# Splitting the recurrence gates' matrix products of the even layer into three rounded products

## The chip, the core and the metric

The kernel runs as one launch on one core of one Trainium2 chip. The metric is the device time of the launch in microseconds (us). Engines are named as the profile names them: PE (TensorE matmuls; PEld is its weight load, which overlaps), DVE (VectorE), ACT (ScalarE), POOL (GpSimd), SP (SyncE, which here only issues transfers from memory).

## The reference, cut to what matters

The program is a stack of four blocks on 512 tokens of width 1024. Only the first one, the even layer, is touched. For each of 8 heads ("channels" here, 128 wide) it projects the normed input six ways, runs a short convolution over one of them (`ua`), makes four gates out of `ua` with 128x128 matrices, and runs a forward and a backward linear recurrence with them:

```python
def rg_lru(u, gate_w, gate_b, lam, reverse):
    uh = uf.reshape(bsz, seq, RG_HEADS, RG_HEAD_DIM)
    gates = sigmoid(einsum('bshi,ghij->gbshj', uh, gate_w) + gate_b)
    r, i = gates[0], gates[1]
    log_a = -RG_C * r * softplus(-lam)
    a = exp(log_a)
    b = sqrt(-expm1(2.0 * log_a)) * (i * uf)
    ...                                   # h_t = a_t h_(t-1) + b_t

def even_layer(x, ...):
    xa, za, xb, gb, gc, zb = split(rmsnorm(x) @ w_in)
    ua = centred_dwconv(xa, conv_w) + conv_b
    ya = (rg_lru(ua, forward) + rg_lru(ua, backward)) * silu(za)
    yb = gb * centred_dwconv(gc * xb, sc_w) * silu(zb)
    y = concatenate([ya, yb]) @ w_out
```

## The kernel before

**Split products.** Nearly all of PE's work is in products of the form hi·w_hi + lo·w_hi + hi·w_lo: a float32 operand is rounded to a high part (type fp32r) and the remainder is its low part. A weight tile of 128x1024 (a "slot") comes through a ring of four slots; POOL makes its high part (`split_slot`, L332, a CAST) and its low part (L334, a TENSOR_TENSOR) in one of two buffer pairs, and counts `w_ready`. PE counts `slots_used` when a slot is through, after which POOL may write that pair again. So POOL works at most two slots ahead of PE. One slot is 8 k-steps of 3 matmuls, 24 in all.

**Channels.** The even layer is a sequence of 8 channels of 6 slots each (slots 0 to 47 below), each slot one projection. PE works through the slots and then through the four gates of the channel, `even_gates` (L654), written before as plain float32 matmuls on `gw` and `ua` (L660). Only channel 0's gates stand later: behind the first slot of channel 1 (L680). ACT moves each projection out of its bank (L1314) in the order xa, xb, gc, gb, zb, za. DVE makes `ua` out of xa (L1763, L1766), then the second convolution (L1790 to L1800); then, when ACT has made the gates' sigmoids and decays (`decay_ready`), the recurrence (L1806 to L1821), and counts `even_channel_done`. Each engine runs its own program in written order; semaphores join them.

**Channel 0** has extra work on DVE between `ua` and the second convolution (`if c == 0:`, L1770): scaling the first banks, norming the input, and a series for the decay constants (`decay_terms`) in tiny operations.

**Channel 7**, the last, has extra work on DVE in the same place (`if last:`, L1786): 14 low parts `y_low_dve` of outputs that are done already, each of which waits for a high part that ACT makes (`y_highs`, L1320) after its last move of this channel.

**After the channels** PE runs the output product (`EVEN_OUT`, L708 to L710). Its first five output tiles leave out the two parts that need channel 7 (`EVEN_K[-2:]`), which come behind those 5 times 14 k-steps.

**Transfers.** SP issues in this order in its loop: wait until the channel two back is done (`even_channel_done`), the gate tile (L590), then the six weight slots (L587), each when the slot before it in the ring was split. So a channel's first weight slots leave only when DVE has finished the channel two earlier.

Of the kernel before, what the change touches and what calls it, by code (L numbers as in the profile page):

```python
# [6 lines left out]
F32 = mybir.dt.float32  # L7
BF16 = mybir.dt.bfloat16
F32R = mybir.dt.float32r
U32 = mybir.dt.uint32  # L10
ACT = mybir.ActivationFunctionType
ALU = mybir.AluOpType
AX = mybir.AxisListType.X

P = 128
D = 1024
T = 512
# [3 lines left out]
RG_HEADS = 8  # L21
# [9 lines left out]
RING = 4  # L31
HALVES = (12, 10)
SLOT = HALVES[0] * P
# [40 lines left out]
GATE_COLS = 4 * P + 16  # L74

SIGNALS = """
const_landed consts_landed out_stored slots_used split_begun w_ready w_cast
masks_zero log_ready nsp_ready plain_high plain_low plain_scaled even_scaled even_high even_low
even_moved ua_ready gates_done gates_read decay_ready factor_ready root_b_ready even_channel_done y_high y_low y_done yb_done
y_moved res_done x_high x_low square_ready square_added sumsq_ready token_sums root_ready rinv_copied token_root token_rinv rinv_ready  # L80
proj_scaled proj_copied r_moved weights_gained v_copied lr_done lr_copied lr_high lr_ready
# [23 lines left out]
def build(nc, x_in, consts_in, gates_in, weights, out):  # L105
    ctx = ExitStack()
    with ctx:
        sem = {}
# [4 lines left out]
        gate_landed = [ctx.enter_context(nc.semaphore(f"gate_landed_{j}")) for j in range(2)]  # L113

        base = (nc.sbuf_base + 31) // 32 * 32
        place = {}
# [6 lines left out]
        def at(name, cols, start, dt=F32):  # L123
            return nc.alloc_sbuf_tensor_at(name, [P, cols], dt, offset=base + 4 * start)

        def tiled(name, n, cols, start, dt=F32):
            return at(name, n * cols, start, dt)[:, :].rearrange("p (k t) -> p k t", t=cols)
# [6 lines left out]
        ARENA_AT = place["arena"]  # L134
# [5 lines left out]
        ring = tiled("ring", RING, SLOT, place["ring"])  # L140
# [271 lines left out]
        r = Region(0, FREE)  # L412
# [12 lines left out]
        nsp = r.take(16)  # L425
        nsp_c = r.tiles(2, 2)
        lt = r.tiles(6, 16)
        even_tmp = [ps[:, 4 + d, :] for d in range(2)]
        rinv_even = ps[:, 6, :]

# [199 lines left out]
        def _(pe):  # L630
# [22 lines left out]

            def even_gates(i, jj):  # L654

                pe.wait_ge(sem["ua_ready"], 2 * i + (jj + 1))
                pe.wait_ge(sem["gates_read"], 2 * i + (jj + 1))
                pe.wait_ge(gate_landed[jj], 16 * i + 16)
                for g in range(4):
                    mm = nc.tensor.matmul(ps[:, 4 + g, :], gw[:, jj, g * P:(g + 1) * P], ua[:, jj, :],  # L660
                                          start=True, stop=True)
                mm.then_inc(sem["gates_done"], 1)

            def even_channel(i, jj, c=None):
# [622 lines left out]
        def _(act):  # L1287
# [15 lines left out]
            def even_act(i, jj, c=None):  # L1303
# [4 lines left out]
                for n, (dst, func) in enumerate(dsts):  # L1308
                    s = 6 * jj + n
                    if c == 0:  # L1310
                        act.wait_ge(sem["plain_scaled"], n + 1)
                    else:
                        act.wait_ge(sem["slots_used"], 12 * i + used("even_in", s + 1))
                    nc.scalar.activation(dst, ps[:, s % RING, :], func).then_inc(sem["even_moved"], 1)  # L1314
                    if c == 0 and n == 3:
                        for k in range(DT):
                            act.wait_ge(sem["even_scaled"], k + 1)
                            nc.scalar.activation(hi[:, k, :], even_tmp[k % 2], ACT.Copy).then_inc(sem["even_high"], 1)
# [365 lines left out]
        def _(dve):  # L1684
# [43 lines left out]
            def even_dve(i, jj, c=None):  # L1728
# [59 lines left out]
                        y_low_dve(n, k)  # L1788
                moved(3)
                V.tensor_tensor(u_pad[:, 1:1 + T], gc_s[:, jj, :], xb_s[:, jj, :], ALU.mult)  # L1790
                dve.drain()
                V.tensor_scalar(cv, u_pad[:, 0:T], par[:, 9:10], None, ALU.mult)
                for k in range(1, 3):
# [566 lines left out]
        def _(pool):  # L2360
# [6 lines left out]
            pool.wait_ge(sem["w_ready"], ready("even_in", 1))  # L2367
            for j in range(1, RING):
                split_slot(pool, "even_in", 0, j)
            with pool.Fori(0, slots_of["even_in"] // RING - 1) as i:  # L2370
                for j in range(RING):
                    split_slot(pool, "even_in", i + 1, j)
            pool.wait_ge(sem["consts_landed"], 16)
            for dst, name in ((ident_1, "ident"), (causal_1, "causal_neg"), (sb_neg_1, "sb_neg"), (neg_c_1, "neg_c")):
                G.tensor_copy(dst, con(name))
# [229 lines left out]
```

## Time and profile before

| | us |
|---|---|
| median of 3 runs (lowest, highest) | 2743.24 (2742.39, 2743.55) |
| the profiled execution | 2743.05 |
| its span | 2741.2 |
| PE busy | 2701.0 |
| POOL busy | 1629.6 |
| DVE busy | 1321.7 |
| ACT busy | 711.8 |

The profiled execution is 1.85 us longer than its span, which is what lies around it. Starts in the trace are counted from the span's start. The even layer's channels lie between 24 and 309 us.

### The profile page before, as it was taken

How to read it: one execution, taken by the hardware profiler on the slowest of the kernel's cores; microseconds unless marked ns; L12 is line 12 of the kernel's file. 1: busy time of each engine (PE TensorE's matmuls, PEld its weight loads, DVE VectorE, ACT ScalarE, POOL GpSimd, SP SyncE). 2: the span in 40 equal slices, each digit the busy share in tenths (PEclk: the TensorE clock that was granted, in tenths of full speed). 3: DMA queues.
4: the chain of work that ended last, by engine and by line, in shares of the span. 5: the costliest groups of instructions: out<-in, count | busy, mean ns of one | idle time of the engine just before them, and what ended most of it. 6: DMA issues, size and time to landing. Idle time of an engine off the chain costs nothing.

```text
span 2741.2 us, 35951 instructions
## 1 busy us (share of the span) xinstructions
PE 2701.0 (99%) x13142; PEld 2166.8 (79%) x13142; DVE 1321.7 (48%) x1601; ACT 711.8 (26%) x1235; POOL 1629.6 (59%) x947
## 2 busy tenths in 40 slices
PE   9999999999999999999999999999999999999999
PEld 6777777867888888867888888788888766888887
DVE  7878824574532461176440433642244777543242
ACT  4433423343200110284210113310011477211010
POOL 5566755514665666603665666566666799566565
PEclk9999999999999999999999999999999999999999
DMA  4322322202332323301332333433232100233232
GB/s 180 101 93 94 90 92 85 84 24 71 96 118 77 96 96 92 93 9 47 92 109 82 100 100 92 125 98 115 77 107 85 55 1 2 85 99 116 77 97 87
DMA packets 62028, 235.58 MB, mean 86 GB/s; under 512 B 6880, under 2 KB 7008, under 8 KB 61792
## 3 DMA queue, kind: packets, MB, share of 16 engines
q1 hardware_dynamic: 61920, 234.14, 27.0%
q8 instruction: 68, 1.11, 0.2%
q14 instruction: 40, 0.33, 0.0%
HBM read 232.02 MB, written 2.10 MB: 85 GB/s over the span
## 4 chain that ended last, share of the span: by engine, by line
PE 81%; DVE 6%; POOL 4%; PEld 3%; ACT 2%; issue 2%; DVEq 1%; PEldq 0%; DMA 0%; POOLq 0%; ACTq 0%; SPq 0%
PE ps L364 23%; PE ps L366 23%; PE ps L365 23%; POOL arena L2430 3%; PE ps L388 1%; PE ps L383 1%; PE ps L382 1%; PE ps L1038 1%; PEld ps L708 1%; PEld ps L709 1%; PEld ps L710 1%; PE ps L1022 1%; PE ps L660 1%; DVE arena L2279 0%; POOL w_lo L334 0%
## 5 line engine op out<-in xcount | busy, mean ns | idle before, releaser
L334 POOL TENSOR_TENSOR w_lo<-ring,w_hi 128x1024 fp32r<-128x1024 f32 (+2 forms) x382 | 992.6, 2598 | 55.1 <-issue 0.2
L332 POOL CAST w_hi<-ring 128x1024 fp32r<-128x1024 f32 (+2 forms) x382 | 436.6, 1143 | 907.1 <-PE ps L366 723.6
L364 PE MATMUL ps<-hi,w_hi 128*128 128x512 f32 x2064 | 810.2, 393 | 5.6 <-POOL w_lo L334 2.9
L366 PE MATMUL ps<-hi,w_lo 128*128 128x512 f32 x2064 | 804.0, 390 | 0.0
L365 PE MATMUL ps<-lo,w_hi 128*128 128x512 f32 x2064 | 803.9, 389 | 0.0
L364 PEld LDWEIGHTS ps<-hi,w_hi 128*128 128x128 f32 x2064 | 388.0, 188 | 92.1 <-POOL w_lo L334 4.8
L365 PEld LDWEIGHTS ps<-lo,w_hi 128*128 128x128 f32 x2064 | 387.9, 188 | 82.3 <-issue 2.6
L366 PEld LDWEIGHTS ps<-hi,w_lo 128*128 128x128 f32 x2064 | 387.9, 188 | 81.2
L364 PE MATMUL ps<-hid_hi,w_hi 128*128 128x512 f32 x704 | 274.4, 390 | 0.0
L365 PE MATMUL ps<-hid_lo,w_hi 128*128 128x512 f32 x704 | 273.9, 389 | 0.0
L366 PE MATMUL ps<-hid_hi,w_lo 128*128 128x512 f32 x704 | 273.9, 389 | 0.0
L2033 DVE TENSOR_TENSOR hid_lo<-arena,hid_hi 128x512 f32 (+1 forms) x88 | 222.2, 2525 | 80.2 <-ACT hid_hi L1505 80.2
L1503 ACT ACTIVATE ps<-ps 128x512 f32<-128x512 f32 x88 | 51.2, 582 | 629.4 <-DVE ps L2025 629.4
L2049 DVE SCALAR_TENSOR_TENSOR res<-ps,res 128x512 f32<-128x512 f32 x64 | 44.3, 691 | 343.8 <-PE ps L366 343.8
L2030 DVE TENSOR_TENSOR arena<-arena,ps 128x512 f32<-128x512 f32 x88 | 60.5, 687 | 275.5 <-PE ps L366 275.0
L1505 ACT ACTIVATE hid_hi<-arena 128x512 f32 (+1 forms) x88 | 55.7, 633 | 410.7 <-DVE arena L2030 410.7
L364 PEld LDWEIGHTS ps<-hid_hi,w_hi 128*128 128x128 f32 x704 | 132.2, 188 | 28.6 <-POOL w_lo L334 1.3
L366 PEld LDWEIGHTS ps<-hid_hi,w_lo 128*128 128x128 f32 x704 | 132.2, 188 | 27.6
L365 PEld LDWEIGHTS ps<-hid_lo,w_hi 128*128 128x128 f32 x704 | 132.2, 188 | 27.2
L2430 POOL TENSOR_SCALAR arena<-arena 128x512 f32<-128x512 f32 (+3 forms) x124 | 133.2, 1099 | 16.9 <-DVE arena L2313 16.7
L246 DVE SCALAR_TENSOR_TENSOR lo<-res,consts,hi 128x512 fp32r<-128x512 f32 x64 | 117.2, 1839 | 32.3 <-ACT hi L240 31.7
L2025 DVE TENSOR_TENSOR ps<-ps,rinv 128x512 f32<-128x512 f32 x88 | 61.5, 699 | 117.8 <-PE ps L366 107.7
(363 smaller groups left out, 3320.4 us busy)
## 6 DMA issues: line engine op xcount, KB each, us to landing
ring<-in_ffn_in SPq DMA_DIRECT2D x176, 512.0 KB, 3.6
ring<-in_even_in SPq DMA_DIRECT2D x48, 512.0 KB, 4.6
ring<-in_ffn_out SPq DMA_DIRECT2D x32, 768.0 KB, 4.3
ring<-in_ffn_out SPq DMA_DIRECT2D x32, 640.0 KB, 3.9
ring<-in_even_out SPq DMA_DIRECT2D x16, 512.0 KB, 3.6
ring<-in_sb_qk SPq DMA_DIRECT2D x12, 512.0 KB, 3.6
ring<-in_odd_v SPq DMA_DIRECT2D x8, 512.0 KB, 3.6
ring<-in_odd_r SPq DMA_DIRECT2D x8, 512.0 KB, 3.6
```

The source lines that it names most:

```text
L246: nc.vector.scalar_tensor_tensor(lo[:, t, :], res[:, t, :], con("g_" + f)[:, t:t + 1], hi[:, t, :].bitcast(F32), ALU.mult, ALU.subtract).t ...
L332: nc.gpsimd.tensor_copy(high[:, j % 2, 0:cols], ring[:, j, 0:cols])
L334: nc.gpsimd.tensor_tensor(low[:, j % 2, 0:cols], ring[:, j, 0:cols], high[:, j % 2, 0:cols].bitcast(F32), ALU.subtract).then_inc(sem["w_re ...
L364: nc.tensor.matmul(bank, w_hi[:, j % 2, w], x_hi[:, k, :], start=(k == 0), stop=False)
L365: nc.tensor.matmul(bank, w_hi[:, j % 2, w], x_lo[:, k, :], start=False, stop=False)
L366: mm = nc.tensor.matmul(bank, w_lo[:, j % 2, w], x_hi[:, k, :], start=False, stop=(k == kt - 1))
L1503: nc.scalar.activation(gate, gate, ACT.Silu).then_inc(sem["silu_done"], 1)
L1505: nc.scalar.activation(hid_hi[:, 2 * i + j, :], wide[:, j, :], ACT.Copy)\
L2025: V.tensor_tensor(gate, gate, rinv[:, :], ALU.mult).then_inc(sem["gate_scaled"], 1)
L2030: V.tensor_tensor(wide[:, j, :], wide[:, j, :], up, ALU.mult).then_inc(sem["hidden_wide"], 1)
L2033: V.tensor_tensor(hid_lo[:, 2 * i + j, :], wide[:, j, :], hid_hi[:, 2 * i + j, :].bitcast(F32), ALU.subtract)\
L2430: op = G.tensor_scalar(part, part, coef[:, s % 4, i, e:e + 1], None, ALU.mult)
```

## The change

Each gate product becomes three rounded ones, as elsewhere in the kernel. POOL gets a `split_gates` that makes the high part of a gate tile in a buffer of its own (`gw_hi`, one for all channels) and writes the low part over the tile itself (`gw_lo`); it stands behind the slot with number 2 or 8 of a group of twelve (in the first group behind slots 3 and 8). ACT makes `ua_hi`; DVE makes `ua_lo`, behind the first operation of the second convolution. PE waits for `gates_split` and `ua_low` instead of `gate_landed` and `ua_ready`.

```diff
@@ PE
             def even_gates(i, jj):
-                pe.wait_ge(sem["ua_ready"], 2 * i + (jj + 1))
                 pe.wait_ge(sem["gates_read"], 2 * i + (jj + 1))
-                pe.wait_ge(gate_landed[jj], 16 * i + 16)
+                pe.wait_ge(sem["gates_split"], 2 * i + (jj + 1))
+                pe.wait_ge(sem["ua_low"], 2 * i + (jj + 1))
                 for g in range(4):
-                    mm = nc.tensor.matmul(ps[:, 4 + g, :], gw[:, jj, g * P:(g + 1) * P], ua[:, jj, :],
-                                          start=True, stop=True)
+                    nc.tensor.matmul(ps[:, 4 + g, :], gw_hi[:, g, :], ua_hi[:, :], start=True, stop=False)
+                    nc.tensor.matmul(ps[:, 4 + g, :], gw_lo[:, jj, g * P:(g + 1) * P], ua_hi[:, :], start=False, stop=False)
+                    mm = nc.tensor.matmul(ps[:, 4 + g, :], gw_hi[:, g, :], ua_lo[:, :], start=False, stop=True)
                 mm.then_inc(sem["gates_done"], 1)
@@ ACT, even_act, in the loop over the six moves n of a channel
                     nc.scalar.activation(dst, ps[:, s % RING, :], func).then_inc(sem["even_moved"], 1)
+                    if n == (1 if c == 0 else 4):
+                        act.wait_ge(sem["ua_ready"], 2 * i + (jj + 1))
+                        nc.scalar.activation(ua_hi[:, :], ua[:, jj, :], ACT.Copy).then_inc(sem["ua_high"], 1)
@@ DVE, even_dve
                 moved(3)
                 V.tensor_tensor(u_pad[:, 1:1 + T], gc_s[:, jj, :], xb_s[:, jj, :], ALU.mult)
+                dve.wait_ge(sem["ua_high"], 2 * i + (jj + 1))
+                V.tensor_tensor(ua_lo[:, :], ua[:, jj, :], ua_hi[:, :].bitcast(F32), ALU.subtract).then_inc(sem["ua_low"], 1)
                 dve.drain()
                 V.tensor_scalar(cv, u_pad[:, 0:T], par[:, 9:10], None, ALU.mult)
@@ POOL
-            with pool.Fori(0, slots_of["even_in"] // RING - 1) as i:
-                for j in range(RING):
-                    split_slot(pool, "even_in", i + 1, j)
+            def split_gates(i, jj):
+                pool.wait_ge(gate_landed[jj], 16 * i + 16)
+                if jj == 1 or not isinstance(i, int):
+                    pool.wait_ge(sem["gates_done"], 2 * i + jj)
+                pool.sem_inc(sem["split_begun"], 1)
+                gates = gw[:, jj, 0:4 * P]
+                nc.gpsimd.tensor_copy(gw_hi[:, :, :].rearrange("p g n -> p (g n)"), gates)
+                pool.drain()
+                nc.gpsimd.tensor_tensor(gw_lo[:, jj, 0:4 * P], gates, gw_hi[:, :, :].rearrange("p g n -> p (g n)").bitcast(F32),
+                                        ALU.subtract).then_inc(sem["gates_split"], 1)
+
+            split_gates(0, 0)
+            for s in range(RING, 12):
+                split_slot(pool, "even_in", s // RING, s % RING)
+                if s == 8:
+                    split_gates(0, 1)
+            with pool.Fori(0, RG_HEADS // 2 - 1) as i:
+                for s in range(12):
+                    split_slot(pool, "even_in", 3 * i + (3 + s // RING), s % RING)
+                    if s in (2, 8):
+                        split_gates(i + 1, s // 6)
```

DVE's program in channel 0, from the end of the series for the decay constants (`arena` holds `ua`, `u_pad` and the constants, `ring` the convolution `cv`), before:

```order
L1782 TENSOR_SCALAR arena<-arena 128x16
L1784 COPY arena<-arena 128x2
L1790 TENSOR_TENSOR arena<-arena 128x512 [waits even_moved]
L1792 TENSOR_SCALAR ring<-arena 128x512
L1795 SCALAR_TENSOR_TENSOR ring<-arena,ring 128x512 x2
```

and now:

```order
L1792 TENSOR_SCALAR arena<-arena 128x16
L1794 COPY arena<-arena 128x2
L1800 TENSOR_TENSOR arena<-arena 128x512 [waits even_moved]
L1802 TENSOR_TENSOR ua_lo<-arena,ua_hi 128x512 [waits ua_high]
L1804 TENSOR_SCALAR ring<-arena 128x512
L1807 SCALAR_TENSOR_TENSOR ring<-arena,ring 128x512 x2
```

The low part of `ua` stands behind the whole series and one product of the second convolution.

DVE's program in channel 7, from the last step of `ua` (`y_lo<-arena,...` are the 14 low parts of finished outputs), before:

```order
L1766 SCALAR_TENSOR_TENSOR arena<-arena 128x512 x3
L1827 TENSOR_TENSOR y_lo<-arena,lo 128x512 [waits y_high] x7
L1827 TENSOR_TENSOR y_lo<-arena,hi 128x512 [waits y_high] x7
L1790 TENSOR_TENSOR arena<-arena 128x512 [waits even_moved]
L1792 TENSOR_SCALAR ring<-arena 128x512
```

and now:

```order
L1776 SCALAR_TENSOR_TENSOR arena<-arena 128x512 x3
L1839 TENSOR_TENSOR y_lo<-arena,lo 128x512 [waits y_high] x7
L1839 TENSOR_TENSOR y_lo<-arena,hi 128x512 [waits y_high] x7
L1800 TENSOR_TENSOR arena<-arena 128x512 [waits even_moved]
L1802 TENSOR_TENSOR ua_lo<-arena,ua_hi 128x512 [waits ua_high]
L1804 TENSOR_SCALAR ring<-arena 128x512
```

`ua` itself still ends ahead of the 14 low parts; its own low part comes behind them.

PE's program at the end of channel 7, where the gates stand between the last slot and the output product, before:

```order
L366 MATMUL ps<-hi,w_lo 128x512
L656 REGISTER_ALU
L660 MATMUL ps<-arena 128x512 [waits gate_landed_1,gates_read,ua_ready]
L660 MATMUL ps<-arena 128x512 x3
L688 REGISTER_ALU
L688 COMPARE_AND_BRANCH
L708 MATMUL ps<-lo,w_hi 128x512 [waits y_low,w_ready,even_moved]
```

and now (of the gates' twelve matmuls the first three):

```order
L366 MATMUL ps<-hi,w_lo 128x512
L662 REGISTER_ALU
L666 MATMUL ps<-ua_hi,gw_hi 128x512 [waits ua_low,gates_split,gates_read]
L667 MATMUL ps<-ua_hi,gw_lo 128x512
L668 MATMUL ps<-ua_lo,gw_hi 128x512
```

The place of the gates in PE's program is the same; what the first of them waits for is another semaphore.

## Rows read from the trace of the kernel before

**Rows 1.** The page's part 1: busy time, share of the span, instructions of each engine.
```profile
PE 2701.0 (99%) x13142; PEld 2166.8 (79%) x13142; DVE 1321.7 (48%) x1601; ACT 711.8 (26%) x1235; POOL 1629.6 (59%) x947
```
**Rows 2.** PE's waits, 40 to 320 us: us in total, times, longest.
```profile
PE ps L364 <- POOL w_lo L334: 2.9, 2, 2.7
```
**Rows 3.** Timeline of PE around channel 2's gates: start, length, engine, line.
```profile
124.07 0.39 PE L366 MATMUL ps<-hi,w_lo 128*128 128x512 f32 x1
124.30 3.59 PE L660 MATMUL ps<-arena 128*128 128x512 f32 x8
...
127.97 0.39 PE L365 MATMUL ps<-lo,w_hi 128*128 128x512 f32 x1
```
**Rows 4.** Timeline, PE at channel 0's gates.
```profile
51.51 3.59 PE L660 MATMUL ps<-arena 128*128 128x512 f32 x8
```
**Rows 5.** Timeline of DVE in channel 0: second convolution, recurrence, end, channel 1's `ua`.
```profile
57.68 0.69 DVE L1790 TENSOR_TENSOR arena<-arena 128x512 f32<-128x512 f32 x1
...
62.73 2.88 DVE L1806 TENSOR_TENSOR w_tails<-arena 128x512 f32<-128x512 f32 x1
...
79.69 0.69 DVE L1821 TENSOR_TENSOR arena<-w_tails,arena 128x512 f32<-128x512 f32 x1
...
80.99 2.42 DVE L1766 SCALAR_TENSOR_TENSOR arena<-arena 128x512 f32<-128x512 f32 x3
```
**Rows 6.** Timeline, 80 to 90 us: SP's gate tile, POOL's split of slot 12.
```profile
80.58 0.35 SPq L590 DMA_DIRECT2D arena<-in_gates  x1
```
```profile
85.74 1.38 POOL L332 CAST w_hi<-ring 128x1024 fp32r<-128x1024 f32 x1 [10.04 <-DMA ring<-in_even_in]
```
**Rows 7.** Timeline of PE at slot 12.
```profile
89.92 0.58 PE L364 MATMUL ps<-hi,w_hi 128*128 128x512 f32 x1 [2.70 <-POOL w_lo L334]
90.29 0.63 PE L365 MATMUL ps<-lo,w_hi 128*128 128x512 f32 x1
...
93.91 0.39 PE L365 MATMUL ps<-lo,w_hi 128*128 128x512 f32 x1
```
**Rows 8.** Windows: busy time of PE, PEld, DVE, ACT, POOL; granted clock, DMA.
```profile
90.00:94.00 4.00, 4.00 (x11) 3.17 (x12) 0.78 (x2) 3.97 (x6) 3.70 (x2) 0.57 0.43 135
...
236.53:272.64 36.11, 36.11 (x154) 28.55 (x153) 28.69 (x24) 14.76 (x20) 23.81 (x13) 1.00 0.29 95
```
**Rows 9.** Timeline of channel 3: DVE's recurrence, SP's gate tile, POOL's slot 24.
```profile
134.32 0.82 DVE L1806 TENSOR_TENSOR w_tails<-arena 128x512 f32<-128x512 f32 x1 [5.33 <-ACT w_tails L1337]
...
151.81 2.62 DVE L1821 TENSOR_TENSOR arena<-w_tails,arena 128x512 f32 x1 [0.17 <-issue]
```
```profile
154.64 0.33 SPq L590 DMA_DIRECT2D arena<-in_gates  x1
```
```profile
160.50 2.61 POOL L334 TENSOR_TENSOR w_lo<-ring,w_hi 128x1024 fp32r<-128x1024 f32 x1
```
**Rows 10.** Timeline of PE at the end of channel 7.
```profile
305.32 3.60 PE L660 MATMUL ps<-arena 128*128 128x512 f32 x8
...
310.21 0.50 PE L708 MATMUL ps<-lo,w_hi 128*128 128x512 f32 x1 [0.60 <-DVE y_lo L1827]
```
**Rows 11.** Timeline of ACT and DVE in channel 7.
```profile
306.02 3.74 ACT L1349 ACTIVATE lo<-arena 128x512 fp32r<-128x512 f32 x7
```
```profile
306.68 6.50 DVE L1827 TENSOR_TENSOR y_lo<-arena,lo 128x512 fp32r<-128x512 f32 x7 [1.57 <-ACT lo L1349]
313.09 4.29 DVE L1827 TENSOR_TENSOR y_lo<-arena,hi 128x512 fp32r<-128x512 f32 x7
317.31 0.68 DVE L1790 TENSOR_TENSOR arena<-arena 128x512 f32<-128x512 f32 x1
...
348.44 0.68 DVE L1827 TENSOR_TENSOR y_lo<-arena,hi 128x512 fp32r<-128x512 f32 x1
```
**Rows 12.** The page's part 5: costliest groups; busy, mean ns, idle before.
```profile
L334 POOL TENSOR_TENSOR w_lo<-ring,w_hi 128x1024 fp32r<-128x1024 f32 (+2 forms) x382 | 992.6, 2598 | 55.1 <-issue 0.2
L332 POOL CAST w_hi<-ring 128x1024 fp32r<-128x1024 f32 (+2 forms) x382 | 436.6, 1143 | 907.1 <-PE ps L366 723.6
```

More of the change, by code:

```diff
@@ L77 @@
 const_landed consts_landed out_stored slots_used split_begun w_ready w_cast
-masks_zero log_ready nsp_ready plain_high plain_low plain_scaled even_scaled even_high even_low
+masks_zero ua_high ua_low gates_split log_ready nsp_ready plain_high plain_low plain_scaled even_scaled even_high even_low
 even_moved ua_ready gates_done gates_read decay_ready factor_ready root_b_ready even_channel_done y_high y_low y_done yb_done
@@ L427, in build @@
         lt = r.tiles(6, 16)
+        r.at = (r.at + P - 1) // P * P
+        gw_hi = tiled("gw_hi", 4, P, ARENA_AT + r.at, F32R)
+        r.take(4 * P)
+        gw_lo = tiled("gw_lo", 2, GATE_COLS, ARENA_AT + 16 * T, F32R)
+        ua_hi = at("ua_hi", T, place["acc"], F32R)
+        ua_lo = at("ua_lo", T, place["ring"] + 3 * SLOT + 8 * P, F32R)
         even_tmp = [ps[:, 4 + d, :] for d in range(2)]
```

## The prediction, made before the changed kernel had run

> **What bounds the kernel now.** I read the page first: PE is busy 99% of the span [rows 1]. So work taken off PE shortens the kernel and a wait put on PE lengthens it, one for one, unless something else is late at that place. PE's waits in the even layer's stretch say how rare that is: one wait of weight for POOL, at slot 12 [rows 2]. The timelines show why even that one exists: the weights of slot 12 leave when DVE has finished channel 0. DVE's last operation there ends at 80.4, SP's gate tile goes at 80.58, POOL starts to split at 85.74, PE starts at 89.92 [rows 5 to 7].
>
> The same chain runs in every channel. Count from T, the moment at which PE has issued the gates of the channel before. For channel 3 T is 127.7 [rows 3]: the next product's second matmul starts at 127.97, one spacing of 0.23 earlier its first is due. DVE starts the recurrence at T+6.6, after ACT's decays, finishes at T+26.7, SP issues, and POOL ends slot 24's low part at 163.1, T+35.4 [rows 9]. A channel takes PE 36.11 [rows 8]. So this chain has only 0.7 us to spare: it is a second bound just under PE.
>
> **What the change takes off PE.** The eight fp32 passes of one channel's gates, from 124.30 to 127.74, take 3.44 [rows 3]. The rounded matmuls stand 0.227 apart (124.07 to 124.30), so twelve of them take 2.73. That is 0.71 less per channel, 5.7 for eight. If that were all, the kernel would take 2743.05 - 5.7 = 2737.4.
>
> The Trainium skill ("TensorE: Matmul & The Clock Gate", section "Wait — 56ns, not 53.3ns?") gives a spacing of 512 ÷ 2.4 GHz + 2.5 ns = 215.8 ns at the full clock; by it the twelve would take 2.59 and the saving would be an estimated 6.8 in all. The rows have 0.227, and nothing below uses the page's figure.
>
> **What it adds, where it is hidden.** POOL: per channel half of a slot's split, by the means 2.60 and 1.14 [rows 12] some 1.3 + 0.57 = 1.9 us. POOL is busy 23.8 of 36.1 [rows 8] and must only be two slots ahead, so as a load this is covered; without the cover it would cost 1.9 per channel. ACT: one copy of 128x512, as in the row of seven in 3.74 some 0.55 to 0.6 [rows 11], on an engine busy 14.8 of 36.1 [rows 8]; in channel 7 it stands ahead of the last move, and I count 0.3 there. DVE: one subtraction, 0.69 if nothing holds it, as L1790 in channel 0; 2.88 if POOL is in the way, as L1806 there [rows 5]. In a middle channel it lies ahead of the recurrence, for which DVE waits 5.33 anyway [rows 9], and is hidden.
>
> **The first wait, in channel 0.** PE reaches these gates at 51.5 [rows 4]. `ua` was long ready. `ua_lo` is not: in DVE's program it stands behind the series and behind L1790, which ends at 58.4 [rows 5]. With a gap of 0.1 and the free 0.69 it ends at 59.1, and PE starts at 59.2: 7.7 late. After an idle of 2.7 the trace shows PE at half its clock (1.2 GHz): granted clock 0.57 of full in 90 to 94, spacing 0.43 [rows 7, 8]. From 89.92 to 93.91 ten spacings took 3.99 instead of 2.28, so a restart costs 1.7. Gates here: 2.73 + 1.7, done at 63.6, against 51.51 + 3.44 = 54.95. PE is 8.7 late.
>
> What is late next is channel 0's end. Before, DVE came to the recurrence at 62.73 from its own work [rows 5]. Now ACT's decays come at 63.6 + 6.6 = 70.2. I take the length of the recurrence from channel 3, 20.1 [rows 9], since POOL's splits now stand to it as there; in channel 0 it took 17.65 (62.73 to 80.38), the other bound. Channel 0 ends at 90.3; slot 12 starts 9.5 later as before (80.38 to 89.92): 99.8, **9.9 late**. Queued behind PE's wait for it are all later slots.
>
> In its shadow lie the gates of channel 1. DVE makes that `ua` only after channel 0's end: 3.0 for `ua` (80.4 to 83.4 now [rows 5]), then L1790 and `ua_lo`, 94.8. PE waits for them from about 91 and issues them at half clock until 99.2. They are hidden, and they take over the restart that slot 12 pays for now: -1.7, so 8.2. Channel 2 then ends, by the chain (99.2 + 35.4 + D, D below) at 135.6 for D = 1, by PE at 99.8 + 24·6·0.227 + 2.73 = 135.2. Slot 18 starts at 135.6 against 127.7: **7.9 late**.
>
> **The middle channels.** PE alone now needs 36.11 - 0.71 = 35.4, exactly what the chain needs already. So the chain decides, with whatever is added to it. `ua_lo` is not in it (it lies ahead of DVE's wait). POOL's gate split is: it comes behind the split of the channel's third slot, at T + 5.4 (24 spacings, until PE frees the buffer) + 3.9 (the split), inside the recurrence, where DVE and POOL hold each other up: L1806 takes 0.69 free and 2.88 under a POOL operation [rows 5]. D, the lengthening, lies between 0 (it falls in gaps that DVE doesn't want) and 1.9 (all of it is waited out). I take 1.0, since of the recurrence's 20.1 about half is operations at their free length and half is being held. Four channels from slot 18 to slot 42: 4 times 36.4, against (272.6 - 127.7) = 144.9 now: +0.7. Bounds: 4·35.4 gives -3.3, 4·37.3 gives +4.3. So the 0.71 per channel is not received.
>
> The Trainium skill ("SBUF — State Buffer", section "SBUF: two separate sides") says of the interfaces that VectorE and GpSimd share that whichever instruction starts first has them for its whole length and the other blocks. By it D would be nearer its upper bound, since each added POOL instruction that starts inside the recurrence is waited out whole; the trace agrees in kind with its 2.88 against 0.69. It is the ground of the second rival.
>
> **The second wait, in channel 7.** PE comes to the gates 13.7 ahead of their operand: it is there at 305.32 [rows 10], while DVE does 14 low parts from 306.68 to 317.38 and L1790 until 318.0 [rows 11]. With 0.3 for ACT's copy and 0.76 for `ua_lo`, 319.05. Nothing on PE can go ahead, since its program is in order and the output product stands behind. Restart at half clock +1.7, gates -0.71, and PE's wait of 0.6 for the second low part at 310.21 [rows 10] falls away: **+14.1**. The output product's two parts that need channel 7 come 70 k-steps (47.8 us) behind its start, that is at about 356.6 before; DVE was done at 349.1 [rows 11]. They move back by no more than the start does, so they stay hidden.
>
> **Sum.** 7.9 + 0.7 + 14.1 = 22.7. Behind the even layer PE is the bound, nothing gives back. 2743.05 + 22.7 = 2765.8; the profiled execution lies 0.2 under the median, which I neglect.
>
> **Rivals.** 0.2% (5.5 us) is about what a measurement of this kernel can tell from no change.
>
> 1. As above, 0.72. Own range 2759 to 2771: D from 0 to 1.9 gives -4.4 and +4.5, and the recurrence of channel 0 at 17.65 or a held `ua_lo` (+2.2) about as much to either side in part.
> 2. The gates' split costs the middle channels all 1.9 and PE's idle at each channel's start (then 1.9 us) brings the half clock each time: 4·(0.9 + 1.7) + 1 = +11, 2777. For it: the mutual holds, and POOL's added work falls inside the recurrence. Against: the drop in the rows came after 2.7 idle. It decides from an idle of somewhere between 0.2 and 2.7. Chance 0.11.
> 3. PE keeps its clock through the waits and channel 0's recurrence takes its old 17.65: 22.7 - 3.4 (the two restarts; the one moved from slot 12 stays away too) - 2.4 = 16.9, and with D = 0 12.5: 2756 to 2760. For it: only one drop is in the trace. Chance 0.11.
> 4. The wait in channel 7 costs nothing, because the output product would have waited for the same 14 low parts anyway: 22.7 - 14.1 - 0.7 = +7.9, 2751. Against: PE waited 0.6 there, at DVE's pace of 0.6 to 0.7 per low part it follows them in step. Chance 0.03.
> 5. The other side: both low parts are made in time and the twelve rounded matmuls bring 5.7, 2737.4. It decides if `ua_lo` ends before 51.5 and 305.3. For it only that DVE has idle elsewhere; its program forbids it in both places. Chance 0.01; the change doing nothing measurable, 0.02.
>
> The range 2757 to 2774 holds 1 and most of 3 and leaves out 2 and the rest. Faster 0.01, same 0.03, slower 0.96.
>
> **What would show it.** PE idle about 7.7 ahead of channel 0's gates with DVE's `ua_lo` as releaser, and 13.7 ahead of channel 7's; the granted clock near half for some 4 us after each; DVE's end of channel 0 near 90; slot starts in the middle 36 to 37 apart, set by POOL's split behind a DMA; the gates at 2.7 where the clock is full; PE's busy time down though the span is longer. The prediction is wrong if `ua_lo` comes earlier than its place in DVE's program says, if the middle channels take 35.4 or more than 37.5, or if the restart costs much more than 1.7.

## The result, and the profile after

| | before | after |
|---|---|---|
| median of 6 runs each (lowest, highest) | 2742.36 (2741.17, 2743.55) | 2766.34 (2765.87, 2772.22) |
| the profiled execution | 2743.05 | 2768.89 |
| its span | 2741.2 | 2767.1 |

The ratio is 1.0091, with a 95% interval of 1.008 to 1.0101: 24.0 us slower, where 2765.8 was predicted. The page's part 1 of the kernel after:

```profile
PE 2704.3 (98%) x13174; PEld 2176.9 (79%) x13174; DVE 1327.1 (48%) x1609; ACT 716.6 (26%) x1243; POOL 1650.8 (60%) x963
```

```profile
PE ps L666 <- DVE ua_lo L1802: 22.5, 3, 13.7
PE ps L364 <- POOL w_lo L334: 6.6, 10, 2.0
```

**Channel 0.** Timeline of PE at the gates (before: [rows 4]): first and last of the twelve, and the product behind them.

```profile
60.99 0.77 PE L666 MATMUL ps<-ua_hi,gw_hi 128*128 128x512 f32 x1 [7.64 <-DVE ua_lo L1802]
61.55 0.63 PE L667 MATMUL ps<-ua_hi,gw_lo 128*128 128x512 f32 x1
...
65.79 0.40 PE L668 MATMUL ps<-ua_lo,gw_hi 128*128 128x512 f32 x1
66.03 0.39 PE L364 MATMUL ps<-hi,w_hi 128*128 128x512 f32 x1
```

Timeline of DVE (before: [rows 5]): `ua_lo` behind the series, the idle time for ACT's decays, the recurrence's first and last operation.

```profile
60.16 0.68 DVE L1802 TENSOR_TENSOR ua_lo<-arena,ua_hi 128x512 fp32r<-128x512 f32 x1
...
72.62 0.78 DVE L1818 TENSOR_TENSOR w_tails<-arena 128x512 f32<-128x512 f32 x1 [8.01 <-ACT w_tails L1347]
...
89.30 0.69 DVE L1833 TENSOR_TENSOR arena<-w_tails,arena 128x512 f32<-128x512 f32 x1
```

The gates take 60.99 to 66.03, 5.04, where 2.73 was predicted at the full clock. The windows of this stretch and of two later ones (us, then busy time of PE, PEld, DVE, ACT and POOL, granted clock, DMA share, GB/s) show where the clock is half:

```profile
60.00:64.00 4.00, 3.01 (x7) 2.46 (x8) 3.60 (x7) 0.00 (x0) 0.00 (x0) 0.50 0.02 4
94.00:98.00 4.00, 3.01 (x12) 2.17 (x12) 3.68 (x5) 1.85 (x3) 2.66 (x2) 1.00 0.95 350
...
330.00:334.00 4.00, 2.35 (x6) 1.91 (x7) 3.68 (x7) 0.00 (x0) 0.00 (x0) 0.50 0.00 0
```

**Channel 1 and slots 12 and 15.** PE's timeline has one short wait ahead of channel 1's gates, then the wait of [rows 7] at slot 12, and at slot 15 one that was not there before:

```profile
94.55 0.47 PE L666 MATMUL ps<-ua_hi,gw_hi 128*128 128x512 f32 x1 [1.14 <-DVE ua_lo L1802]
99.52 0.50 PE L364 MATMUL ps<-hi,w_hi 128*128 128x512 f32 x1 [1.96 <-POOL w_lo L334]
119.04 0.50 PE L364 MATMUL ps<-hi,w_hi 128*128 128x512 f32 x1 [1.29 <-POOL w_lo L334]
```

The gates there ran at the full clock (second window above). What POOL does before slot 15, in its timeline:

```profile
108.46 2.65 POOL L334 TENSOR_TENSOR w_lo<-ring,w_hi 128x1024 fp32r<-128x1024 f32 x1
111.06 1.08 POOL L2388 CAST gw_hi<-arena 128x512 fp32r<-128x512 f32 x1
112.28 2.02 POOL L2390 TENSOR_TENSOR gw_lo<-arena,gw_hi 128x512 fp32r<-128x512 f32 x1
114.25 1.50 POOL L332 CAST w_hi<-ring 128x1024 fp32r<-128x1024 f32 x1
115.89 3.09 POOL L334 TENSOR_TENSOR w_lo<-ring,w_hi 128x1024 fp32r<-128x1024 f32 x1
```

The gate split takes 3.2 here from its start to its end, and at the start of the kernel 2.05:

```profile
28.27 0.61 POOL L2388 CAST gw_hi<-arena 128x512 fp32r<-128x512 f32 x1
29.02 1.30 POOL L2390 TENSOR_TENSOR gw_lo<-arena,gw_hi 128x512 fp32r<-128x512 f32 x1
```

**Channel 7.** Timelines of PE, of ACT and of DVE (before: [rows 10, 11]):

```profile
331.65 0.77 PE L666 MATMUL ps<-ua_hi,gw_hi 128*128 128x512 f32 x1 [13.69 <-DVE ua_lo L1802]
...
336.23 0.40 PE L715 MATMUL ps<-lo,w_hi 128*128 128x512 f32 x1
```
```profile
319.76 0.63 ACT L1324 ACTIVATE ua_hi<-arena 128x512 fp32r<-128x512 f32 x1 [6.59 <-DVE arena L1776]
```
```profile
313.65 6.08 DVE L1776 SCALAR_TENSOR_TENSOR arena<-arena 128x512 f32<-128x512 f32 x3
321.42 4.67 DVE L1839 TENSOR_TENSOR y_lo<-arena,lo 128x512 fp32r<-128x512 f32 x7 [1.70 <-ACT lo L1359]
326.02 4.29 DVE L1839 TENSOR_TENSOR y_lo<-arena,hi 128x512 fp32r<-128x512 f32 x7
...
330.83 0.68 DVE L1802 TENSOR_TENSOR ua_lo<-arena,ua_hi 128x512 fp32r<-128x512 f32 x1
```

**One difference between the two traces also occurs without the change.** Slot 2 starts at 24.96 after and at 23.28 before:

```profile
24.96 0.47 PE L364 MATMUL ps<-y_lo,w_hi 128*128 128x512 f32 x1 [0.48 <-POOL w_lo L334]
```
```profile
23.28 0.47 PE L364 MATMUL ps<-y_lo,w_hi 128*128 128x512 f32 x1 [0.49 <-POOL w_lo L334]
```

In the traces of the experiments below slot 2 starts near 23.4 or between 24.8 and 25.3 (once at 26.1) whatever the edit, and the one experiment on the kernel before is among the later ones (25.09). So these 1.68 are taken off wherever stages are compared, though two traces of the kernel before can't show that the change leaves the odds of a late start alone; behind slot 2 the change shows as follows (before to after, 1.68 taken off):

| stage | before | after | own shift, in all |
|---|---|---|---|
| channel 0's gates done | 54.95 | 66.03 | +9.4 |
| slot 12 starts | 89.92 | 99.52 | +7.9 |
| slot 18 starts | 127.7 | 138.2 | +8.8 |
| slot 42 starts | 272.64 | 284.72 | +10.4 |
| output product starts | 308.76 | 336.23 | +25.8 |
| 112 of its 128 k-steps done | 388.60 | 414.03 | +23.7 |

Each stage is read from one execution. The kernel of experiment 2 below has the same program up to channel 7, and its trace differs: slot 12 starts 72.4 behind slot 2 (74.6 in the kernel after), slot 18 starts 36.7 behind that (38.7), the four middle channels take 147.6 (146.5), and PE's wait at slot 15 is half as long:

```profile
114.44 0.50 PE L364 MATMUL ps<-hi,w_hi 128*128 128x512 f32 x1 [0.62 <-POOL w_lo L334]
```

So a single stage between slots 2 and 42 is known to about 1 to 2 us only.

### The profile page after: what moved, and what is told of

Its sections match the earlier page's. It is cut to its first block, busy times and chain, and to the rows that moved or that the text cites. A ratio compares the mean times of both kernels' runs of the same rounds, so it can differ in the third digit from the quotient of the medians.

```text
span 2767.1 us, 36043 instructions
## 1 busy us (share of the span) xinstructions
PE 2704.3 (98%) x13174; PEld 2176.9 (79%) x13174; DVE 1327.1 (48%) x1609; ACT 716.6 (26%) x1243; POOL 1650.8 (60%) x963
## 4 chain that ended last, share of the span: by engine, by line
PE 78%; DVE 6%; POOL 4%; PEld 4%; ACT 2%; issue 2%; POOLq 1%; DVEq 1%; DMA 1%; PEldq 0%; ACTq 0%; SPq 0%
PE ps L364 22%; PE ps L365 22%; PE ps L366 22%; POOL arena L2460 3%; PE ps L388 2%; PE ps L382 2%; PE ps L383 2%; PE ps L1045 1%; PEld ps L715 1%; POOL w_lo L334 1%; PEld ps L716 1%; PEld ps L717 1%; DVE w_tails L1829 1%; POOLq L333 1%; DVE w_tails L1820 1%
## 5 line engine op out<-in xcount | busy, mean ns | idle before, releaser
L246 DVE SCALAR_TENSOR_TENSOR lo<-res,consts,hi 128x512 fp32r<-128x512 f32 x64 | 104.5, 1640 | 31.9 <-ACT hi L240 31.7
```

The lines of the kernel that those rows point to most:

```text
L246: nc.vector.scalar_tensor_tensor(lo[:, t, :], res[:, t, :], con("g_" + f)[:, t:t + 1], hi[:, t, :].bitcast(F32), ALU.mult, ALU.subtract).t ...
```

## The experiments

The times are medians, with the lowest and highest run. The ratio is to the kernel before, run beside each (medians 2742.2 to 2743.5); "after" is the changed kernel at 2766.34. Since the kernel before itself moved by 1.3 from one set of runs to another, a difference against after is uncertain by about 1 us.

### 1 to 3: `ua_lo` where `ua` ends, in channel 0, in channel 7, in both

```diff
+                def low_u():
+                    dve.wait_ge(sem["ua_high"], 2 * i + (jj + 1))
+                    V.tensor_tensor(ua_lo[:, :], ua[:, jj, :], ua_hi[:, :].bitcast(F32), ALU.subtract)\
+                        .then_inc(sem["ua_low"], 1)
...
                 # behind the last step of ua, ahead of the series (c == 0) and of the 14 low parts (last)
+                early = c == 0                  # second: c == RG_HEADS - 1; third: either
+                if early:
+                    low_u()
```

> Channel 0's low part of ua is made right behind ua, ahead of the scaling, norming and series. My theory (PE waits in program order for a late ua_lo in channels 0 and 7): the wait of 7.6 us and the restart at half clock ahead of channel 0's gates go, slot 12 starts near 90 as in the kernel before, everything behind is 7 to 9 us earlier, 2757 to 2759. Rival (the time is lost to POOL's added split and the holds between DVE and POOL): the wait is replaced by another, under 3 us gained, 2764 or more.

> The same in channel 7 only: ua_lo ahead of the 14 low parts of finished outputs. My theory: the wait of 13.7 goes down to 3 to 4 us, because ua itself ends about 2 us behind PE's last slot there and its two halves take 1.4 more; the output product then starts 10 to 12 us earlier, 2754 to 2757. Rival 1 (the output product would wait for the same low parts anyway): PE waits at its first products instead, 2763 or more. Rival 2 (POOL's added split): as for channel 0.

> Both edits. My theory: the two add, 2766.3 - 8 - 11 = 2747 (2744 to 2750), that is still a little over the kernel before, by what the middle channels lose. Rival (a shared cause, such as the chain of transfers behind DVE's end of a channel): they don't add, 2752 or more.

| kernel | median (lowest, highest) | to before | against after |
|---|---|---|---|
| channel 0 alone | 2762.67 (2762.22, 2766.92) | 1.0079 [1.0065, 1.0093] | -3.7 |
| channel 7 alone | 2755.34 (2752.47, 2760.31) | 1.0052 [1.0038, 1.0065] | -11.0 |
| both | 2751.35 (2750.45, 2755.13) | 1.0038 [1.0025, 1.0052] | -15.0 |

Channel 7 came at the time expected: PE's wait falls from 13.69 to 1.90, further than the 3 to 4 of the expectation.

```profile
316.97 0.47 PE L666 MATMUL ps<-ua_hi,gw_hi 128*128 128x512 f32 x1 [1.90 <-DVE ua_lo L1767]
```

Channel 0 gave half of what was expected, a time between the ranges of theory and rival. Its wait is gone (the gates start at 52.57), but PE now waits at slot 10 for a bank, so a wait was replaced by another, as the rival has it, though not by one for POOL. In the kernel before the same wait for ACT was 1.13 (at 72.60), which the prediction didn't look at. Timelines of PE, DVE and ACT of the kernel with channel 0 alone:

```profile
78.24 0.79 PE L364 MATMUL ps<-hi,w_hi 128*128 128x512 f32 x1 [6.46 <-ACT arena L1321]
```
```profile
68.39 2.88 DVE L1826 TENSOR_TENSOR w_tails<-arena 128x512 f32<-128x512 f32 x1
```
```profile
77.07 0.63 ACT L1354 ACTIVATE ring<-w_tails 128x512 f32<-128x512 f32 x1 [4.37 <-DVE w_tails L1828]
77.61 2.04 ACT L1321 ACTIVATE arena<-ps 128x512 f32<-128x512 f32 x4
```

ACT's four moves of channel 1 stand behind its two square roots of channel 0, which wait for DVE's recurrence; DVE begins that at 68.39 instead of 62.73 [rows 5]. The trace shows two parts of this: the low part of `ua` and DVE's wait for its high part took 1.45, and the two steps of the convolution took 3.55 beside POOL's split of a slot (62.48 to 64.88), where they took 1.58 before. In the kernel after, PE's 7.6 us ahead of the gates had hidden this second delay. Both edits together give the sum of the two (-3.7 - 11.0 = -14.7; measured -15.0).

### 4: POOL's gate split one slot earlier

```diff
-                    if s in (2, 8):
+                    if s in (1, 7):
```

> The changed kernel, only POOL's gate split stands behind the second slot of a channel instead of the third, where DVE idles ahead of the recurrence. My theory (in its place now the split lengthens the recurrence and delays POOL's next slot: PE waits of 1.0 to 1.3 in three channels): channels from slot 18 on start 35.4 to 35.7 apart instead of 36.6 on the mean, 3 to 5 us earlier, 2761 to 2763. Rival (only the amount of POOL's work counts, wherever it stands): 2766, same as the changed kernel.

2762.19 (2760.84 to 2763.76), 1.0071 [1.0057, 1.0085]: -4.1, the time expected. From slot 12 to slot 18 it takes 36.0 instead of 38.7, and the four middle channels 145.1 instead of 146.5 (147.6 in experiment 2): 36.3 each, where 35.4 to 35.7 was expected. POOL's split of the gates of channel 2 now lies at 102.99 to 105.95, in time in which POOL waited for PE before (3.34 us, up to 107.04, in the kernel after), and the wait at slot 15 is gone.

### 5 and 6: SP sends a channel's first weights before it waits for DVE

```diff
-                            sp.wait_ge(sem["even_channel_done"], 2 * i + (jj + 3))
-                            gate_weight(i + 1, jj)
...                             # now ahead of the third of the channel's six slots
+                                if n == 2:
+                                    sp.wait_ge(sem["even_channel_done"], 2 * i + (jj + 3))
+                                    gate_weight(i + 1, jj)
```

The fifth kernel is the one before with this edit, the sixth the one after.

> The kernel before, only SP's order changed: a channel's first two weight slots are issued ahead of the wait for the end of the channel two back and of the gate tile. My theory (a chain from DVE's end of a channel over SP and POOL sets the start of the next but one channel, with 0.7 us to spare, and alone makes the wait at slot 12): the wait of 2.7 at slot 12 and its restart at half clock (1.7) go, and 0.4 at slot 30: 2742.2 - 4.8 = 2737.4 (2736.5 to 2739). Rival (slot 12 waits for something else late there too, such as ACT's moves): 2740 or more.

> The same edit of SP's order on the changed kernel. My theory: the waits at slot 12 and at the channels' starts (0.15 each) go and the middle channels lose only the 1.0 to 1.3 that POOL's gate split costs at the fourth slot; 3 to 5 us under the changed kernel, 2761.5 to 2763.5. Rival (the gate split alone holds the middle channels): 2765 or more.

| kernel | median (lowest, highest) | to before |
|---|---|---|
| on the kernel before | 2746.27 (2745.68, 2748.44) | 1.0013 [1.0004, 1.0022] |
| on the kernel after | 2805.25 (2805.11, 2806.56) | 1.0226 [1.0212, 1.024] |

Both expectations were wrong, the second by over 40 us. SP's wait for DVE was taken for a cost; it keeps POOL away from DVE. Timelines of the sixth kernel at channel 3: PE, DVE and POOL.

```profile
186.54 0.76 PE L667 MATMUL ps<-ua_hi,gw_hi 128*128 128x512 f32 x1 [5.25 <-DVE ua_lo L1803]
```
```profile
177.82 5.23 DVE L1777 SCALAR_TENSOR_TENSOR arena<-arena 128x512 f32<-128x512 f32 x3
182.97 2.83 DVE L1801 TENSOR_TENSOR arena<-arena 128x512 f32<-128x512 f32 x1
185.72 0.68 DVE L1803 TENSOR_TENSOR ua_lo<-arena,ua_hi 128x512 fp32r<-128x512 f32 x1
```
```profile
181.47 1.04 POOL L332 CAST w_hi<-ring 128x1024 fp32r<-128x1024 f32 x1 [1.48 <-PE ps L366]
182.65 2.60 POOL L334 TENSOR_TENSOR w_lo<-ring,w_hi 128x1024 fp32r<-128x1024 f32 x1
```

The three steps of `ua` take 5.23 with POOL at work and 2.42 without it [rows 5], the product behind them 2.83 instead of 0.69. PE waits 5.25 for `ua_lo`, falls to half its clock and needs 5.26 for the gates (186.54 to 191.80 in PE's timeline). A channel takes 43 to 44 us instead of 36.6. In the fifth kernel the same happened once, at channel 1's gates (its middle channels are at 36.11 as before):

```profile
90.45 1.22 PE L661 MATMUL ps<-arena 128*128 128x512 f32 x1 [4.86 <-DVE arena L1767]
```

### 7: float32 gate products of the high parts alone

This kernel has all waits, copies and splits of the change, but computes the gates as four float32 products; the low parts are left out of the computation.

```diff
-                    nc.tensor.matmul(ps[:, 4 + g, :], gw_hi[:, g, :], ua_hi[:, :], start=True, stop=False)
-                    nc.tensor.matmul(ps[:, 4 + g, :], gw_lo[:, jj, g * P:(g + 1) * P], ua_hi[:, :], start=False, stop=False)
-                    mm = nc.tensor.matmul(ps[:, 4 + g, :], gw_hi[:, g, :], ua_lo[:, :], start=False, stop=True)
+                    mm = nc.tensor.matmul(ps[:, 4 + g, :], gw_hi[:, g, :].bitcast(F32), ua_hi[:, :].bitcast(F32),
+                                          start=True, stop=True)
```

> The changed kernel with its splits and waits, but the gates are again plain float32 products, here of the high parts alone, so that the low parts are left out of the computation. It prices the saved passes where they stand now. My theory (only channels 0, 7 and partly the middle ones receive the 0.71, the rest is under the chain): 1.5 to 4 us over the changed kernel, 2768 to 2770. Rival (TensorE is the bound in every channel): all eight, +5.7 and more at half clock, 2772 or more.

2770.56 (2769.87 to 2771.15), 1.0099 [1.0084, 1.0115]: +4.2 over the kernel after, of the 5.7 of work on PE that the edit puts back (just above the expected 2768 to 2770). In the four middle channels it takes 148.4, against 146.5 in the kernel after and 147.6 in experiment 2: 0.8 to 1.9 of the 2.8 that 4 times 0.71 would be. So a good part of the 0.71 per channel is received after all.

### 8 and 9: the edits together

Both have `ua_lo` early in channels 0 and 7 (in channel 0 behind the scaling and norming, ahead of the series) and the gate split at (1, 7); the eighth also has SP's weights first.

> The changed kernel with four edits: ua_lo ahead of the series in channel 0 and ahead of the 14 low parts in channel 7, POOL's gate split behind the second slot of a channel, SP's first two weight slots ahead of its wait. My theory (nothing but order costs time, the rounded products are worth 0.71 per channel once nothing stands over them): 2742.2 - 4.8 (as in the kernel before with SP's edit) - 5 (seven channels) + 1.5 (channel 0's later recurrence) + 2 (PE's wait for ua_lo in channel 7) = 2736 (2733 to 2739). Rival (the mutual holds of DVE and POOL cost what the passes save): 2740 or more.

> The changed kernel with three of the four edits; SP's order is as it was, so that POOL again has no weights while DVE makes the next ua. My theory, formed after the last runs (POOL's wait for weights is what leaves DVE free for ua; with the weights early DVE is held and ua_lo comes 1 us late in each channel): the waits of 1.0 ahead of the gates go, channels stand 36.1 apart instead of 36.65, against that slot 12 waits for its transfer again; 2744 to 2748, under the kernel with four edits. Rival (SP's chain cost time and its removal was a gain): 2750 or more. In neither case under the kernel before by more than 1.

| kernel | median (lowest, highest) | to before |
|---|---|---|
| four edits | 2748.43 (2746.55, 2749.91) | 1.0019 [1.001, 1.0028] |
| three, without SP's | 2745.34 (2743.12, 2746.95) | 1.001 [1.0001, 1.002] |

The eighth was expected at 2736 on the same belief about SP as the fifth and sixth, and fell with it; its middle channels take 36.65 each, and PE waits for `ua_lo` in seven of the eight channels, 7.1 us in all.

The ninth was expected at 2744 to 2748 and is there. It takes back 21.0 of the 24.0. Its largest wait is the one at slot 10:

```profile
77.17 0.80 PE L364 MATMUL ps<-hi,w_hi 128*128 128x512 f32 x1 [5.88 <-ACT arena L1321]
```

### 10: POOL's high part of the gate tile made twice

```diff
                 nc.gpsimd.tensor_copy(gw_hi[:, :, :].rearrange("p g n -> p (g n)"), gates)
                 pool.drain()
+                nc.gpsimd.tensor_copy(gw_hi[:, :, :].rearrange("p g n -> p (g n)"), gates)
+                pool.drain()
```

> The changed kernel, but POOL makes the high part of each gate tile twice (one more 128x512 CAST of 0.6 to 1.1 us with its drain per channel, the result is the same). Theory (POOL's gate split stands in the middle of DVE's recurrence and ahead of a slot that PE needs soon, so each us there goes through to PE in the middle channels): 0.7 to 1.3 for each of five to six channels, 4 to 7 us over the changed kernel, 2770 to 2773. Rival (POOL has 12 idle us per channel that take it up): 2768 or less.

2768.60 (2766.70 to 2773.49), 1.0092 [1.0078, 1.0105]: +2.3 over the kernel after, between the rival's range and the 4 to 7 of the theory, so the times decide for neither. Its trace, of its slowest run, shows where more of POOL's work does become PE's wait: in each of the five channels from slot 18 on PE waits 1.14 or 1.15 for POOL at the fourth slot (0.15 to 0.18 in the kernel after), and the four middle channels take 148.7, against 146.5 there and 147.6 in experiment 2. The wait at slot 15 is 2.18, but that one differs by 0.7 between executions of the same program.

### 11: keeping PE at work while it waits in channel 0

```diff
+                if isinstance(i, int) and jj == 0:
+                    for n in range(32):
+                        nc.tensor.matmul(ps[:, 4, 0:P], ones, ones, start=True, stop=True)
```

> The changed kernel, but PE fills its wait ahead of channel 0's gates with 32 small float32 matmuls into a bank that the gates overwrite, some 7 us of work. Theory (after an idle of 7.6 PE restarts at half clock, 5.0 for the twelve matmuls instead of 2.7): the gates take 2.7, channel 0's decays and end come 2.3 earlier and slot 12 with them; 2763.5 to 2765. Rival (the restart is in the shadow of the chain over DVE and POOL): gates at full clock but 2766, no change.

2765.89 (2763.18 to 2767.09), 1.0083 [1.007, 1.0097]: 0.45 below the kernel after, which the spreads don't tell from nothing. The trace shows the mechanism: PE's timeline, and the clock in the window of the gates.

```profile
51.55 7.31 PE L665 MATMUL ps<-consts 128*128 128x128 f32 x64
59.13 0.47 PE L669 MATMUL ps<-ua_hi,gw_hi 128*128 128x512 f32 x1 [0.27 <-DVE ua_lo L1805]
```
```profile
59.00:63.00 4.00, 3.87 (x17) 3.23 (x18) 3.37 (x5) 0.83 (x2) 0.71 (x1) 1.00 0.00 0
```

The gates take 2.84 (59.13 to 61.97) instead of 5.04, and slot 12 starts 72.1 behind slot 2 instead of 74.6. That last comparison proves little, since the trace of experiment 2 has 72.4 without the filling. Why the median keeps so little of the gates' 2.2 was not settled; the executions differ by more than that up to slot 18.

### 12: the three edits, with the gate split of channel 1 behind slot 11

```diff
-                if s == 8:
+                if s == 11:
                     split_gates(0, 1)
```

> The kernel with three edits (2745.3 us), but channel 0 splits the gate tile of channel 1 behind its weight slot 11 instead of 8. In the trace of the three edits that split lay at 55.4 to 57.5, on the vector engine's series of channel 0, and the recurrence began at 67.5. Theory, that the split behind slot 8 is what holds the series there: the recurrence begins 1 to 2 us earlier, the wait of 5.9 us at slot 10 for the scalar engine's move of channel 1's input falls to 4 to 5, and the time is 2743 to 2745. Rival, that the hold only moves: the split then lies at about 75 to 78 on the recurrence's last updates, which wait up to 1.9 us, and the time is 2745 to 2747.

2745.94 (2744.42 to 2746.98), 1.0008 [0.9999, 1.0017]: no better than the ninth, as the rival has it, although the theory's first two steps came and more. The recurrence starts 42.3 behind slot 2 instead of 44.1, and slot 10's wait falls to 1.86. What was won is then waited for at the gates of channel 1 and slot 12:

```profile
75.00 0.50 PE L364 MATMUL ps<-hi,w_hi 128*128 128x512 f32 x1 [1.86 <-ACT arena L1321]
88.64 0.47 PE L666 MATMUL ps<-ua_hi,gw_hi 128*128 128x512 f32 x1 [2.46 <-DVE ua_lo L1767]
93.60 0.50 PE L364 MATMUL ps<-hi,w_hi 128*128 128x512 f32 x1 [1.96 <-POOL w_lo L334]
```

The second half of the recurrence and POOL's split of the gates, in the timelines of DVE and POOL:

```profile
75.32 2.74 DVE L1835 TENSOR_TENSOR w_tails<-arena,ring 128x512 f32<-128x512 f32 x1
78.14 1.48 DVE L1838 TENSOR_TENSOR_SCAN w_tails<-arena,w_tails 128x512 f32<-128x512 f32 x1
```
```profile
77.46 1.08 POOL L2397 CAST gw_hi<-arena 128x512 fp32r<-128x512 f32 x1
78.68 2.02 POOL L2399 TENSOR_TENSOR gw_lo<-arena,gw_hi 128x512 fp32r<-128x512 f32 x1
```

The first of these takes 2.74 beside POOL's split of a slot (74.84 to 77.51). Beside the gate split the scan takes 1.48 instead of 1.23, and the product behind it (L1835 again) 1.56, where the same product takes 0.69 in the kernel after (L1826, at 81.75). The recurrence takes 16.6 instead of 14.7 in the ninth. From slot 2 to slot 18 the two kernels take the same, 105.5 and 105.6.

## Why the prediction was right, step by step

**The two waits carry it.** PE's waits of 7.64 and 13.69 stand where 7.7 and 13.7 were predicted, released by `ua_lo`, and experiments 1 to 3 undo them: with both gone the kernel is 15.0 faster. The late `ua_lo` is thus the cause of at least that much of the 24.

**Channel 0, +8.7: +9.4.** The wait was right to 0.1; the term that was too small is the restart at half clock, 1.7 by the restart of slot 12, 2.3 here (5.04 - 2.73). In channel 7 it took 1.85 (331.65 to 336.23, less 2.73). Experiment 11 shows that it is the clock: with PE at work until 0.3 before them, the same twelve take 2.84.

**Slot 12, +9.9: +7.9.** Too large by 2.0. The chain's pieces were right: decays to recurrence 6.6 (66.03 to 72.62), channel end to slot 12 9.5 (89.99 to 99.52). The length of the recurrence was taken from channel 3, 20.1, with 17.65 as the other bound; it was 17.4. The reason given, that POOL's splits would stand to it as in channel 3, was wrong: POOL had split everything in the ring by 87.4, since SP still waited for this same recurrence, and DVE's last two products ran free (0.69 each).

**Slot 18, +7.9: +8.8.** The step that failed is that channel 1's gates would run at half clock and take the restart over from slot 12 (-1.7). PE waited 1.14 for them and kept the full clock; then it waited 1.96 at slot 12 and lost it, as before. In the other direction stands the wait of 1.29 at slot 15, which no term had: of 38.70 - 37.81 = +0.89, it is +1.29, the gates are -0.71, and 0.3 is left. The load on POOL was called covered because it "must only be two slots ahead". It is not covered right after slot 12, where POOL has no slot ready and must first win its lead back, and where the gate split costs 3.2 instead of 1.9 with DVE at work beside it. Experiment 4 bears this out: one slot earlier the wait is gone and the median falls by 4.1. How much of it is lost differs: in experiment 2 the wait was 0.62.

**The middle channels, +0.7: +1.6** (146.50 against 144.91). The sum came out near, but by two errors that cancel. The first is D, the lengthening of the chain, taken as 1.0 between 0 and 1.9. DVE's recurrence between slots 24 and 30, timeline of its first and last operation:

```profile
180.67 0.69 DVE L1818 TENSOR_TENSOR w_tails<-arena 128x512 f32<-128x512 f32 x1 [0.60 <-ACT w_tails L1347]
...
200.15 2.63 DVE L1833 TENSOR_TENSOR arena<-w_tails,arena 128x512 f32 x1 [0.17 <-issue]
```

It takes 22.1 here (180.67 to 202.78), 21.7 to 22.2 in four channels, instead of 20.1 [rows 9]. The chain from the issued gates (174.08) to slot 30 (211.53) takes 37.45 instead of 35.4. So D was 1.6 to 2.0. By the Trainium skill ("SBUF — State Buffer", section "SBUF: two separate sides") D had to be nearer to 1.9, as each POOL instruction that starts in the recurrence is waited out whole. The trace agrees in size, though the holds are not all whole: beside the gate split in experiment 12 one DVE product took 1.56 instead of 0.69.

The second error is the step "four channels: 4 times 36.4", which charges D to every channel in full. PE issues a channel's gates and only then waits for the next slot, so the next recurrence starts ahead of that wait. The channels took 37.1, 36.2, 37.2 and 36.0, with waits of 1.06 and 1.04 for POOL at slots 24 and 36 and about 0.3 at slot 30: per channel some half of D comes through, 36.6 on the mean. The sentence "the 0.71 per channel is not received" was too strong for the same reason: experiment 7 gives back 0.8 to 1.9 of 2.8 in these channels when the saving is taken away.

**Channel 7, +14.1: +15.4 to the start of the output product, 13.3 behind it.** The wait was 13.69, though by two errors that cancel. The first low part of the outputs began 3.6 behind the moment at which PE could have issued the gates (321.42 against 317.81) instead of 1.4 [rows 10, 11]: the recurrence of channel 6 had ended 1.1 nearer to that moment, and the three steps of `ua` took 6.08 beside POOL, where they took 5.08 before (300.02 to 305.10). And the first seven low parts took 4.67 instead of 6.50 [rows 11]. Of the 15.4, 13.69 - 0.71 + 1.85 = 14.8 are the step's, 0.6 came before the gates. In the output product 2.1 are given back: the waits of 0.6 and 0.8 that PE had there for DVE and POOL before are gone, where 0.6 was predicted, and the 0.7 left is in the spacings around them.

**Sum.** 22.7 predicted; own shift 23.7 in the traces, 24.0 in the medians. The errors (+0.7, -2.7, +2.9 up to slot 18, +0.9, -0.8) cancel in good part, so the centre owes something to luck; the two waits do not. The own shift ends at 24.2 by the spans (25.9 - 1.68). That it meets the 24.0 of the medians is luck too: where slot 2 starts in the executions without a trace isn't known.

**Rivals.** The second had the middle channels at D = 1.9 and a half clock at each start. Its D came, but not its channels of 37.3, and not its clock, as the window from slot 18 to slot 42 shows:

```profile
138.22:284.72 146.50, 143.65 (x626) 116.59 (x625) 132.75 (x94) 61.58 (x84) 104.76 (x56) 1.00 0.27 90
```

The third had no drop of the clock; there were two new ones. The fourth, that the wait in channel 7 costs nothing, is refuted by experiment 2, where its removal gains 11.0. The fifth needed `ua_lo` in time; it was not, and even with it early in both channels (experiment 9) the kernel is at 2745.34, not 2737.4.

**What stays open.** Experiment 9 is still 2.6 above before, not faster. Its waits show where: 5.88 at slot 10 for ACT, and 0.7 to 1.9 at four places for POOL and `ua_lo`. Whether the 5.88 can be had by moving ACT's moves ahead of its square roots was not tried. What decides whether PE keeps its full clock over an idle of some 2 us stays open too (below). No run here beats the kernel before.

## What to carry to other kernels

A finer split of an operand moves work to other engines and adds a semaphore: ask first where in its engine's written order the new operand's maker stands, since PE here waited 21 us at two places for a low part whose maker stood behind other work. In channel 0 `ua` had long been ready; in channel 7 it ended 1.8 behind PE's last slot, and its low part another 11.8 later. Before taking away a wait, look at what the waiting engine would do in that time and whom it would hold: SP's wait for the recurrence looked like the chain's slack, and without it the changed kernel was 39 us slower, the kernel before 3.4. When one wait is removed, read what was hidden in its shadow: of 7.6 us at channel 0's gates 6.5 came back at slot 10.

## What the runs showed of the hardware

- Two engines slowed each other in both directions. POOL's cast and subtraction of 128x512 took 0.61 and 1.30 alone and 1.08 and 2.02 beside DVE's recurrence; DVE's three scalar_tensor_tensor steps took 2.4 alone and 4.4 to 6.1 beside POOL's splits.
- PE had the half clock after idles of 1.96, 5.25, 7.64 and 13.69 us. It kept the full clock over 1.14 ahead of channel 1's gates, over 1.90 in experiment 2 (316.97) and over 2.46 in experiment 12 (88.64). In experiment 9, behind the same 1.90 ahead of channel 7's gates (308.35), six matmuls ran at the full clock and the next eight at a spacing of 0.43. So the length of one idle doesn't tell: the prediction's "between 0.2 and 2.7" is no bound that holds each time. The half clock then cost 1.8 to 2.5 us in twelve matmuls. With 7.31 us of small matmuls in the wait of channel 0 it stayed full.
- The start of the program differed by some 1.7 us between profiled executions of like kernels. In the execution of after PE's clock was half from 14 to 18, ahead of everything that the change touches; in the kernel before it was full there (1.00), and in experiment 5, on the kernel before, 0.63:

```profile
14.00:18.00 4.00, 4.00 (x12) 3.05 (x12) 3.82 (x7) 0.62 (x2) 0.00 (x0) 0.57 1.10 454
```
